# Attention values for 256 queries in one step, gate work at the end of a unit, expert gate-and-up weights in two halves

## The chip, the cores and the metric

One core of one Trainium2 chip runs the whole program. The metric is the device time of one execution in microseconds (us), lower is better. The engines are TensorE (PE, with its weight loads PEld), VectorE (DVE), ScalarE (ACT), GpSimd (POOL) and SyncE (SP), which issues the large transfers.

## What is computed

Two layers of a mixer block run on 512 rows of x and 256 rows of context, then a second block (dilated and forgetting attention, then a mixture of 32 experts). The change touches two parts. The first is the attention of the two mixer layers:

```python
def one_block(qi):                      # 128 queries; 8 heads
    s = jnp.einsum('bqhd,bkhd->bhqk', qi, k).astype(jnp.float32) * sm_scale
    p = jax.nn.softmax(s, axis=-1).astype(v.dtype)
    return jnp.einsum('bhqk,bkhd->bqhd', p, v)
...
y_a = attn * jax.nn.silu(g_a)
```

Its keys are the 256 context rows and the 512 rows of x; in layer 0 the context rows are queries too, against the context alone. The second is the experts:

```python
for e in range(N_EXPERTS):              # 32 experts, 1024 -> 256 -> 1024
    he = jax.nn.silu(xt @ w_gate[e]) * (xt @ w_up[e])
    y = y + combine[:, e:e + 1] * (he @ w_down[e])
```

## The kernel before

Every engine runs its own list of instructions in order, and all five lists come from one walk that each engine's code goes through with its own functions. Between engines there are counted semaphores; there is no scheduler, so the order in the walk is the order on the engine.

**Attention.** A *unit* is one head and 128 queries: five units per head in layer 0 (`per = 5`; the fifth, `i == 4`, is the 256 context queries against the 256 context keys) and four in layer 1; 40 and 32 units in all. `attention_walk` goes through the units u. For each it calls, in this order: `values` of an earlier unit if one is due at u, `turn_p(u)` (TensorE turns the softmax weights P, six transposes of 128x128, DVE and ACT copy them to PTa/PTb/PTc), a piece of turning the next heads' q or k, `normalise(u+2)` (DVE reciprocal, POOL multiply), `scores(u+3)` (TensorE q·k, DVE maximum, ACT exponential), and `finish` (DVE's low parts of turned q and k). Heads go in pairs, an even and an odd one. `values` multiplies PT with v for the two heads of a pair: the even head's result lands in rows 0 to 63 and the odd head's in rows 64 to 127 of one PSUM place, and the `due` table says at which unit each step stands. In `values`, DVE multiplies the place with the gate (L1687, into `og`), ACT copies the result to the high part `yax` or `yac` (L1634), and POOL makes the low part (L1717).

**PSUM places.** `K.G` is a ring of four places of 512 columns, made in `attention_pe`. Each P piece (two per unit, one for `i == 4`), each turned piece of q or k, and each step of values takes the next place in turn. A taker waits until the last user's reader is done: for a place of values that is DVE's gate multiplication, event `gated`. The scores have two places of their own, used alternately.

**Experts.** The experts go in 16 pairs. For a pair, TensorE multiplies 64 rows each with the gate-and-up weights `gu` (L3421, 8 row blocks k, two experts beside each other in the columns of the array), turns the result and multiplies with `dn` (L3444). Six `gu` buffers of 2 MB and eight `dn` buffers of 1 MB form rings. SP issues one transfer per buffer (`experts_load`), each after the last user is done (`weight_free`) and after the fourth load before it has landed.

Of the kernel before, what the change touches and what calls it, by code (L numbers as in the profile page):

```python
# [15 lines left out]
NX = 512  # L16
# [251 lines left out]
def setup(K, nc):  # L268
# [16 lines left out]
    for l, a in ((0, 0), (1, 50)):  # L285
# [14 lines left out]
            (f"P{l}", 4 * row, a + 30, a + 30), (f"PTa{l}", 12 * kb, a + 30, a + 30), (f"PTb{l}", 6 * kb, a + 30, a + 30),  # L300
            (f"PTc{l}", 4 * kb if l == 0 else 32, a + 30, a + 30), (f"og{l}", 3 * kb, a + 30, a + 30),
# [4 lines left out]
        if l == 0:  # L306
            items += [("zero", 4 * kb, 30, 30), ("yac0", 8 * kb, 30, 42), ("ysc0", 4 * kb, 20, 42), ("ypc0", 4 * kb, 24, 42)]
# [1105 lines left out]
def attention_walk(S, l, turn=nothing, rest=nothing, scores=nothing, normalise=nothing, turn_p=nothing, values=nothing):  # L1413
# [47 lines left out]
def attention_buffers(K, l):  # L1461
# [6 lines left out]
    A.P, A.PT = ring("P", 4, (NT,)), (ring("PTa", 4, (6, 128)), ring("PTb", 2, (6, 128)))  # L1468
    A.PTc = ring("PTc", 2, (2, 256)) if l == 0 else None
    A.gate = ring("og", 3, (256,))  # L1470
# [3 lines left out]
    def pt(u):  # L1474

        h, i = units[u]
        if i == 4:
            return A.PTc[h % 2], u - 2 * per + per * (1 - h % 2)
        if h % 2 == 0:
            return A.PT[0][i], u - per  # L1480
        return A.PT[1][i % 2], u - 2 if i >= 2 else u - 2 * per + 2
# [59 lines left out]
def attention_pe(S, l):  # L1541
# [40 lines left out]
    def values(u):  # L1582
        h, i = units[u]
        s, before = K.G.take("gated", l, u)
        n, kts = (128, range(6)) if i < 4 else (NC, (4, 5))
        for kt in kts:
            for odd in range(2):
                of = u - per * (1 - odd)
                o = 64 * (h - 1 + odd)
                for w in q(*[("pt", l, of, j) for j in range(len(A.jobs(of)))], *[("v", l, t) for t in range(6)], *before):  # L1590
# [11 lines left out]
def attention_act(S, l):  # L1602
# [25 lines left out]
    def values(u):  # L1628
        h, i = units[u]
        c, n = 128 * i % NX, 128 if i < 4 else NC  # L1630
# [4 lines left out]
    attention_walk(S, l, turn=turn, scores=scores, turn_p=turn_p, values=values)  # L1635
# [8 lines left out]
def gate_of(A, u):  # L1644

    h, i = A.units[u]
    return (h // 2 * A.per + i) % 3


def attention_dve(S, l):  # L1650
# [29 lines left out]
    def values(u):  # L1680
        h, i = units[u]
        c, n = 128 * i, 128 if i < 4 else NC
        g = gate_of(A, u)
        earlier = [v for v in range(u) if units[v][0] % 2 and gate_of(A, v) == g]
# [3 lines left out]
    attention_walk(S, l, rest=rest, scores=scores, normalise=normalise, turn_p=turn_p, values=values)  # L1688


def attention_pool(S, l):
# [3 lines left out]
    if l == 0:  # L1695
        zero = K.sb("zero", [128, D])
# [14 lines left out]
    def values(u):  # L1711
        h, i = units[u]
        c, n = 128 * i % NX, 128 if i < 4 else NC
# [4 lines left out]
    attention_walk(S, l, normalise=normalise, values=values)  # L1718


def attention_sp(S, l):
    K, e, q = S.K, S.e, S.q
    if l == 0:
        for w in q(("zeros",)):
            e.wait_ge(*w)
        e.dma_start(K.ybuf.rearrange("(p c) n -> p c n", c=8), K.sb("zero", [128, D])[:, :].unsqueeze(1).to_broadcast([128, 8, D])).then_inc(*q.land("zero"))
# [10 lines left out]
def y_ready(l, v, k, part):  # L1737
# [4 lines left out]
    return [(("yah", "yal")[part], l, per * (2 * k + 1) + i) for i in (range(4) if v == 0 else (4,))]  # L1742
# [1310 lines left out]
def experts_load(S, n):  # L3053
    K, e, q = S.K, S.e, S.q
    for i in range(S.loaded, S.loaded + n):
        w, x = EXPERT_LOADS[i]
        for s in q(*weight_free(w, x), *([("w", *EXPERT_LOADS[i - 4])] if i > 3 else [])):
            e.wait_ge(*s)
        b = weight_place(K, w, x)
        e.dma_start(b[:, :, :], K.d["w_" + w][x]).then_inc(*q.land_as(f"{w}{x % (N_GU if w == 'gu' else N_DN)}", "w", w, x))  # L3060
# [40 lines left out]
def weights_of(K, E, job):  # L3101

    kind, n = job
    if kind == "far":
        return [(E.w_gu, ("second.far_gu", n), E.w_dn, ("second.far_dn", n))]
    return [(weight_place(K, "gu", x), ("w", "gu", x), weight_place(K, "dn", x), ("w", "dn", x)) for x in (2 * n, 2 * n + 1)]
# [283 lines left out]
def experts_pe(S):  # L3390
# [21 lines left out]
    def up(job, xt, j, free):  # L3412
# [3 lines left out]
        for k in range(KT):  # L3416
            for i, (gu, loaded, _, _) in enumerate(ws):
                o = slice(n * i, n * i + n)
                for w in q(ev("XT", job, 0), ev("XT", job, 1), loaded, *before):
                    e.wait_ge(*w)  # L3420
                m = e.matmul(s[o, :], x[:, k, o], gu[:, k, :], start=k == 0, stop=k == KT - 1, skip_group_check=True)  # L3421
                if k == KT - 1 and i == len(ws) - 1:
                    m.then_inc(*q.up(*ev("up", job)))
# [479 lines left out]
```

## Time and profile before

| what | value |
|---|---|
| median of 3 runs | 1336.57 us (1335.91 to 1337.82) |
| profiled execution, its own time | 1337.34 us |
| its span in the trace | 1335.5 us |
| mean granted TensorE clock | 0.985 of full speed |
| busy: PE, DVE, ACT, POOL | 96%, 50%, 39%, 40% of the span |

The profile is of one execution; its own time is 0.77 us above the median. Busy time is what the hardware recorded on each engine. A matmul's end is modelled, and in an unbroken stream the next one starts before the modelled end of the last, so distances from start to start are the safer reading. An fp32 matmul shows as two records. The two attentions lie at about 280 to 391 us and 626 to 721 us, the experts at 1070 to 1306 us.

### The profile page before, as it was taken

How to read it: one execution, taken by the hardware profiler on the slowest of the kernel's cores; microseconds unless marked ns; L12 is line 12 of the kernel's file. 1: busy time of each engine (PE TensorE's matmuls, PEld its weight loads, DVE VectorE, ACT ScalarE, POOL GpSimd, SP SyncE). 2: the span in 40 equal slices, each digit the busy share in tenths (PEclk: the TensorE clock that was granted, in tenths of full speed). 3: DMA queues.
4: the chain of work that ended last, by engine and by line, in shares of the span. 5: the costliest groups of instructions: out<-in, count | busy, mean ns of one | idle time of the engine just before them, and what ended most of it. 6: DMA issues, size and time to landing. Idle time of an engine off the chain costs nothing. (4 is left out here: it accounts for less than half of the span.)

```text
span 1335.5 us, 20477 instructions
## 1 busy us (share of the span) xinstructions
PE 1277.2 (96%) x7788; PEld 925.0 (69%) x7788; DVE 662.2 (50%) x1358; ACT 524.9 (39%) x1121; POOL 538.9 (40%) x552
## 2 busy tenths in 40 slices
PE   7999999999999999999999999999989989989995
PEld 6766777878888878667888987767668933333332
DVE  5555995147741587973774331544454511111125
ACT  4312343357652344434665333655452221111111
POOL 0213698344445446874334521665261101111121
PEclk9999999999999999999999999999999799999998
DMA  9782111140013231022001222221046779999985
GB/s 395 302 295 95 48 47 48 48 158 2 1 48 111 80 117 63 32 79 80 2 1 47 82 95 87 81 102 48 32 158 254 297 291 419 422 419 416 418 346 210
DMA packets 42513, 209.58 MB, mean 157 GB/s; under 512 B 7255, under 2 KB 9687, under 8 KB 33184
## 3 DMA queue, kind: packets, MB, share of 16 engines
q1 hardware_dynamic: 34192, 194.59, 37.5%
q0 software_dynamic: 5760, 10.27, 2.1%
q10 hardware_dynamic: 2448, 3.21, 0.8%
q8 instruction: 71, 1.16, 0.4%
q14 instruction: 42, 0.34, 0.1%
HBM read 201.46 MB, written 17.30 MB: 164 GB/s over the span
## 5 line engine op out<-in xcount | busy, mean ns | idle before, releaser
L438 POOL TENSOR_TENSOR wlo<-raw,whi 128x512 fp32r<-128x512 f32 x102 | 141.3, 1389 | 140.8 <-ACT whi L426 135.8
L3421 PE MATMUL ps<-gu,XT 128*64 128x512 f32 x608 | 135.7, 595 | 8.6 <-DVE XT L3533 5.1
L426 ACT ACTIVATE whi<-raw 128x512 fp32r<-128x512 f32 x124 | 76.8, 629 | 149.1 <-PE ps L881 112.3
L1165 DVE SCALAR_TENSOR_TENSOR z<-glu,small,z 128x798 f32<-128x798 f32 (+1 forms) x120 | 132.5, 1153 | 0.8
L881 PE MATMUL ps<-hxh,whi 128*128 128x512 f32 x304 | 129.3, 425 | 0.5 <-ACT whi L426 0.5
L881 PE MATMUL ps<-hxh,wlo 128*128 128x512 f32 x304 | 120.1, 395 | 2.1 <-POOL wlo L438 2.1
L881 PE MATMUL ps<-hxl,whi 128*128 128x512 f32 x304 | 120.6, 397 | 0.0
L3421 PEld LDWEIGHTS ps<-gu,XT 128*64 128x64 f32 x608 | 45.0, 137 | 86.7 <-issue 75.9
L1708 POOL TENSOR_SCALAR P<-P,stat 128x768 f32<-128x768 f32 (+1 forms) x80 | 65.5, 821 | 72.2 <-DVE stat L1670 71.1
L1617 ACT ACTIVATE P<-ps,stat 128x768 f32<-128x768 f32 (+1 forms) x80 | 65.1, 814 | 59.0 <-DVE stat L1663 58.3
L1663 DVE TENSOR_REDUCE stat<-ps 128x1 f32<-128x768 f32 (+1 forms) x72 | 66.6, 925 | 22.5 <-PE ps L1568 22.2
L3538 DVE TENSOR_TENSOR he<-ps,he 128x256 f32<-128x256 f32 x19 | 8.1, 424 | 137.6 <-ACT he L3499 137.6
L881 PEld LDWEIGHTS ps<-hxh,whi 128*128 128x128 f32 x304 | 57.8, 190 | 22.9 <-issue 9.6
L3444 PE MATMUL ps<-dn,heT 128*64 128x512 f32 x304 | 69.4, 598 | 3.5 <-DVE heT L3543 3.5
L881 PEld LDWEIGHTS ps<-hxh,wlo 128*128 128x128 f32 x304 | 57.5, 189 | 15.6 <-POOL wlo L438 2.5
L881 PEld LDWEIGHTS ps<-hxl,whi 128*128 128x128 f32 x304 | 57.7, 190 | 14.1 <-issue 2.2
L3499 ACT ACTIVATE he<-ps 128x256 f32<-128x256 f32 x19 | 7.3, 383 | 149.8 <-PE ps L3421 149.8
L1578 PE MATMUL ps<-ident,P 128*128 128x128 f32 x416 | 61.3, 283 | 1.2 <-DVE qT_1l L1525 0.5
L3615 POOL DMA_INDIRECT h<-h2d,kept x16 | 16.3, 1020 | 110.8 <-PE ps L3408 77.1
L2525 POOL TENSOR_SCALAR P<-P,stat 128x128 f32<-128x128 f32 (+3 forms) x64 | 35.1, 559 | 49.9 <-DVE stat L2471 49.9
L2221 PE MATMUL ps<-hh,whi 128*128 128x512 f32 x128 | 55.1, 430 | 0.0
L1578 PEld LDWEIGHTS ps<-ident,P 128*128 128x128 f32 x416 | 47.4, 143 | 10.6 <-issue 5.9
(849 smaller groups left out, 3189.2 us busy)
## 6 DMA issues: line engine op xcount, KB each, us to landing
gu<-in_w_gu_dram SPq DMA_DIRECT2D x32, 2048.0 KB, 16.4
raw<-in_w_in_dram SPq DMA_DIRECT2D x66, 512.0 KB, 3.3
dn<-in_w_dn_dram SPq DMA_DIRECT2D x32, 1024.0 KB, 16.5
wgate<-in_w_mod_dram SPq DMA_DIRECT2D x16, 1024.0 KB, 7.8
raw<-in_w_out_dram SPq DMA_DIRECT2D x24, 512.0 KB, 3.2
wmod<-in_w_mod_dram SPq DMA_DIRECT2D x4, 2048.0 KB, 14.9
ybuf<-zero SPq DMA_DIRECT2D x1, 4096.0 KB, 12.7
yin<-ybuf SPq DMA_DIRECT2D x4, 1024.0 KB, 9.4
```

The lines of the kernel that those rows point to most:

```text
L426: e.activation(K.hi[i][:, half(h)], K.raw[i % 2][:, half(h)], ACT.Copy).then_inc(*q.up("hi", i, h))
L438: e.tensor_tensor(K.lo[i][:, half(h)], K.raw[i % 2][:, half(h)], K.hi[i][:, half(h)].bitcast(F32), ALU.subtract).then_inc(*q.up("lo", i, h))
L881: p = e.matmul(s[0:m, o:o + n], a, K.h[l, v][x][:, k, :], start=k == 0 and part == 0 and x == 0, stop=end)
L1165: e.scalar_tensor_tensor(o, x, weight, o, ALU.mult, ALU.add).then_inc(*q.up("conv", l, i, j))
L1578: m = e.transpose(s[:, 128 * j:128 * j + 128], A.P[u % 4][:, c:c + 128], K.ident[:, :])
L1617: e.activation(P[:, wide * j:wide * j + wide], s[:, wide * j:wide * j + wide], ACT.Exp, bias=K.stat[:, c0 + j:c0 + j + 1], accum_out=K.sta ...
L1663: e.tensor_reduce(stat[:, c0:c0 + n], A.S[u % 2][:, 0:n * wide].rearrange("p (n w) -> p n w", w=wide), AX.X, ALU.max, negate=True).then_in ...
L1708: e.tensor_scalar(P[:, wide * j:wide * j + wide], P[:, wide * j:wide * j + wide], K.stat[:, c0 + 4 + j:c0 + 5 + j], 0.0, ALU.mult, ALU.add ...
L2221: m = e.matmul(s[:, :], (K.hi, K.lo)[part][i][:, 128 * k:128 * k + 128], K.h[2, 0][x][:, k, :], start=k == 0 and part == 0 and x == 0, sto ...
L2525: e.tensor_scalar(P[:, 0:n], P[:, 0:n], stat[:, c0 + 3:c0 + 4], 0.0, ALU.mult, ALU.add).then_inc(*q.up("normal2", u))
L3421: m = e.matmul(s[o, :], x[:, k, o], gu[:, k, :], start=k == 0, stop=k == KT - 1, skip_group_check=True)
L3444: m = e.matmul(s[o, :], turned_of(E, job)[:, k, o], dn[:, k, 512 * c:512 * c + 512], start=k == 0, stop=k == 1, skip_group_check=True)
```

## The change

Four things are changed in the attentions, and one in the experts.

1. One step of `values` now serves two units, that is 256 queries: units i = 0 and 1, or i = 2 and 3 of both heads. The context unit i = 4 stays a step of its own. PT tiles are 256 queries wide (two for each head instead of 4 and 2 of 128), and so are the gate tiles `og`, two instead of three.
2. The steps stand at other units: at 8, 10 and 12 of each ten in layer 0 (before 6, 8, 10, 12 and 14), at 7 and 9 of each eight in layer 1 (before 5, 7, 9 and 10).
3. The gate work on DVE, ACT and POOL is no longer done where `values` stands, but by a new call `gate` after `scores(u+3)` of the same unit.
4. The tile of zeros is 256 columns wide instead of 1024, and its transfer reads it more often.
5. Each `gu` buffer is loaded by two transfers of 1 MB (row blocks 0 to 3, and 4 to 7). The first may start when the first half of the pair's multiplication is done (`up_half`), and the multiplication waits for each half by itself.

```diff
-            (f"P{l}", 4 * row, a + 30, a + 30), (f"PTa{l}", 12 * kb, a + 30, a + 30), (f"PTb{l}", 6 * kb, a + 30, a + 30),
-            (f"PTc{l}", 4 * kb if l == 0 else 32, a + 30, a + 30), (f"og{l}", 3 * kb, a + 30, a + 30),
+            (f"P{l}", 4 * row, a + 30, a + 30), (f"PTa{l}", 12 * kb, a + 30, a + 30), (f"PTb{l}", 12 * kb, a + 30, a + 30),
+            (f"PTc{l}", 4 * kb if l == 0 else 32, a + 30, a + 30), (f"og{l}", 2 * kb, a + 30, a + 30),
...
-    due = {2 * per * p + d: 2 * per * p + per + i for p in range(HEADS // 2) for i, d in enumerate((6, 8, 10, 12, 14) if l == 0 else (5, 7, 9, 10))}
+    due = {2 * per * p + d: 2 * per * p + per + i for p in range(HEADS // 2) for i, d in (((1, 8), (3, 10), (4, 12)) if l == 0 else ((1, 7), (3, 9)))}
...
-        if u in due:
-            values(due.pop(u))
+        own = due.pop(u, None)
+        if own is not None:
+            values(own)
         turn_p(u)
...
         if u + 3 < n:
             scores(u + 3)
+        if own is not None:
+            gate(own)
         finish()
     for u in sorted(due):
         values(due[u])
+        gate(due[u])
...
+def value_part(A, u):
+    i = A.units[u][1]
+    return (128 * i - 128, 256, [u - 1, u]) if i < 4 else (NX, NC, [u])
...
-        n, kts = (128, range(6)) if i < 4 else (NC, (4, 5))
+        kts = range(6) if i < 4 else (4, 5)
+        _, n, own = value_part(A, u)
         for kt in kts:
             for odd in range(2):
-                of = u - per * (1 - odd)
+                of = [v - per * (1 - odd) for v in own]
+                p = A.PT[odd][i // 2] if i < 4 else A.PTc[odd]
...
-                m = e.matmul(s[64 * odd:64 * odd + 64, 0:n], B.vN[:, kt, o:o + 64], A.pt(of)[0][:, kt - kts[0], :],
+                m = e.matmul(s[64 * odd:64 * odd + 64, 0:n], B.vN[:, kt, o:o + 64], p[:, kt - kts[0], :],
...
-    attention_walk(S, l, rest=rest, scores=scores, normalise=normalise, turn_p=turn_p, values=values)
+    attention_walk(S, l, rest=rest, scores=scores, normalise=normalise, turn_p=turn_p, gate=values)
...
-def weight_free(w, x):
+def weight_free(w, x, part=1):
+    up = ("up_half", "up")[part]
...
-        return [("first.up", p), ("second.up", p)] if w == "gu" else [("first.down", p, 1), ("second.down", p, 1)]
+        return [("first." + up, p), ("second." + up, p)] if w == "gu" else [("first.down", p, 1), ("second.down", p, 1)]
...
+        rows = slice(KT // 2 * part, KT // 2 * part + KT // 2)
+        e.dma_start(b[:, rows, :], K.d["w_gu"][x][:, rows, :]).then_inc(*q.land_as(f"gate{x % N_GU}" if part == 0 else f"gu{x % N_GU}", *(("w", "gu", x) if part else ("w_half", "gu", x))))
...
-                for w in q(ev("XT", job, 0), ev("XT", job, 1), loaded, *before):
+                for w in q(ev("XT", job, 0), ev("XT", job, 1), loaded[k // (KT // 2)], *before):
```

On DVE, in layer 0, this stood in unit 8, which begins with a step of values (`og0_1` is the gate tile, `PTb0_1` the copy of the unit's P, `stat_60` holds reciprocal and maximum, `kT0_1l` a turned piece of k):

```order
L1687 TENSOR_TENSOR og0_1_240<-ps,ga0_214 128x128 [waits s_pe_attention]
L1678 COPY PTb0_1_236<-ps 128x512 [waits s_pe_attention]
L1670 RECIPROCAL stat_60<-stat_60 128x1 [waits s_act_attention]
L1663 TENSOR_REDUCE stat_60<-ps 128x1 [waits s_pool_attention,s_pe_attention]
L1525 SCALAR_TENSOR_TENSOR kT0_1l_226<-ps,small_54,kT0_1h_225 96x512 [waits s_act_attention]
```

and this stands there now:

```order
L1690 COPY PTb0_1_234<-ps 128x4x128 [waits s_pe_attention]
L1682 RECIPROCAL stat_60<-stat_60 128x1 [waits s_act_attention]
L1675 TENSOR_REDUCE stat_60<-ps 128x1 [waits s_pool_attention,s_pe_attention]
L1699 TENSOR_TENSOR og0_0_237<-ps,ga0_214 128x256
L1528 SCALAR_TENSOR_TENSOR kT0_1l_226<-ps,small_54,kT0_1h_225 96x512 [waits s_act_attention]
```

The gate multiplication moved from the unit's beginning to behind the maximum of scores(u+3), and is twice as wide.

TensorE's list from the end of that step of values into unit 9 reads now as follows (L1597 values, L1581 transposes of P, L1505 transposes of k, L1571 scores; each piece of P or k takes one of the four places):

```order
L1597 MATMUL ps<-PTb0_0_233,vN0_218 64x256
L1581 MATMUL ps<-ident_49,P0_0_227 128x128 [waits s_dve_attention,s_pool_attention]
L1581 MATMUL ps<-ident_49,P0_0_227 128x128 x3
L1581 MATMUL ps<-ident_49,P0_0_227 128x128 [waits s_act_attention]
L1581 MATMUL ps<-ident_49,P0_0_227 128x128
L1505 MATMUL ps<-ident_49,kN0_217 96x128 [waits s_dve_attention]
...
L1571 MATMUL ps<-kT0_0h_223,qT0_0l_220 128x512
L1571 MATMUL ps<-kT0_0h_223,qT0_0l_220 128x256
L1581 MATMUL ps<-ident_49,P0_1_228 128x128 [waits s_dve_attention,s_pool_attention]
```

The rows are those of before but for the 256 columns of the values; what moved is the instruction behind the last wait on DVE: the transposes of P0_1 take the fourth place after the values, which is the values' own, and its reader is now the gate multiplication at the end of unit 8.

SP's list of loads in the experts had, where the rings begin to be reused:

```order
L3060 DMA gu0_348<-in_w_gu_dram 128x4096 [waits s_gu4,s_pe_second,s_pe_first]
L3060 DMA gu1_350<-in_w_gu_dram 128x4096 [waits s_dn6]
L3060 DMA gu2_352<-in_w_gu_dram 128x4096 [waits s_gu5,s_pe_second,s_pe_first]
L3060 DMA gu3_354<-in_w_gu_dram 128x4096 [waits s_dn7]
L3060 DMA dn0_349<-in_w_dn_dram 128x2048 [waits s_gu0,s_pe_second,s_pe_first]
```

and has now:

```order
L3082 DMA gu0_342<-in_w_gu_dram 128x2048 [waits s_gu4,s_pe_second,s_pe_first]
L3082 DMA gu1_344<-in_w_gu_dram 128x2048 [waits s_dn6]
L3082 DMA gu0_342<-in_w_gu_dram 128x2048 [waits s_pe_second,s_pe_first]
L3082 DMA gu1_344<-in_w_gu_dram 128x2048
L3082 DMA gu2_346<-in_w_gu_dram 128x2048 [waits s_gu5,s_pe_second,s_pe_first]
```

Both first halves of a pair go ahead of both second halves.

## Rows read from the trace of the kernel before

**Rows 1.** The page: busy time of the engines; TensorE's granted clock.

```profile
PE 1277.2 (96%) x7788; PEld 925.0 (69%) x7788; DVE 662.2 (50%) x1358; ACT 524.9 (39%) x1121; POOL 538.9 (40%) x552
...
PEclk9999999999999999999999999999999799999998
```

**Rows 2.** Windows: 20 units of layer 0, 16 units of layer 1.

```profile
core 0: us, PE busy (x) PEld busy (x) DVE busy (x) ACT busy (x) POOL busy (x), PEclk, DMA share, GB/s
300.43:354.50 54.07, 53.41 (x490) 46.32 (x489) 40.62 (x85) 37.94 (x95) 23.26 (x34) 1.00 0.01 2
644.69:690.25 45.56, 45.29 (x426) 39.48 (x425) 33.66 (x68) 30.07 (x69) 18.19 (x25) 1.00 0.01 1
```

**Rows 3.** Timeline of PE: values for 128 and for the context.

```profile
start us, us, engine line op out<-in xcount [idle before <-releaser]
305.69 0.51 PE L1568 MATMUL ps<-kT_0h,qT_0l 96*128 96x512 f32 x2
306.13 0.32 PE L1592 MATMUL ps<-PTa,vN 128*64 128x128 f32 x1
...
307.59 0.87 PE L1578 MATMUL ps<-ident,P 128*128 128x128 f32 x6
...
322.60 1.08 PE L1592 MATMUL ps<-PTc,vN 128*64 128x256 f32 x8
323.61 0.66 PE L1578 MATMUL ps<-ident,P 128*128 128x128 f32 x4
```

**Rows 4.** Waits before L1592 (all its steps), and one such step on PE.

```profile
  ACT PTb L1626: 3.7, 8
...
711.49 0.43 PE L1592 MATMUL ps<-PTa,vN 128*64 128x128 f32 x2
712.68 0.29 PE L1592 MATMUL ps<-PTb,vN 128*64 128x128 f32 x1 [0.76 <-ACT PTb L1626]
...
714.11 0.33 PE L1578 MATMUL ps<-ident,P 128*128 128x128 f32 x1
```

**Rows 5.** Timeline of PE and of DVE where scores end.

```profile
309.44 0.51 PE L1568 MATMUL ps<-kT_0h,qT_0l 96*128 96x512 f32 x2
309.79 0.60 PE L1578 MATMUL ps<-ident,P 128*128 128x128 f32 x4
310.23 0.38 PE L1502 MATMUL ps<-ident,kN 128*96 128x128 f32 x2
...
309.99 0.96 DVE L1663 TENSOR_REDUCE stat<-ps 128x1 f32<-128x768 f32 x1 [0.94 <-PE ps L1568]
```

**Rows 6.** Groups by line and form on DVE: gate and maximum.

```profile
L1687 DVE TENSOR_TENSOR og<-ps,ga 128x128 f32<-128x128 f32 x32 | 9.1, 286 | 11.1 <-PE ps L1592 11.1
L1687 DVE TENSOR_TENSOR og<-ps,ga 128x256 f32<-128x256 f32 x4 | 1.7, 416 | 0.6 <-PE ps L1592 0.6
L1663 DVE TENSOR_REDUCE stat<-ps 128x1 f32<-128x768 f32 x64 | 61.1, 954 | 21.2 <-PE ps L1568 20.8 <-issue 0.3
```

**Rows 7.** The chain that ended last: from DVE's end to TensorE's start.

```profile
1309.23 0.43 DVE heT L3543
1309.66 0.04 issue
1309.71 3.68 PE ps L3444 x16
```

**Rows 8.** Windows around two idle stretches of TensorE; columns as in rows 2.

```profile
286.00:289.00 3.00, 1.66 (x10) 1.09 (x8) 1.94 (x4) 1.19 (x3) 0.90 (x1) 1.00 1.02 412
289.00:293.00 4.00, 3.51 (x20) 3.46 (x19) 3.27 (x8) 2.54 (x6) 1.25 (x2) 0.57 1.03 417
...
1179.00:1182.00 3.00, 0.55 (x3) 0.20 (x4) 0.06 (x1) 0.00 (x0) 1.01 (x1) 1.00 1.02 419
1182.00:1185.00 3.00, 3.00 (x16) 1.01 (x14) 0.00 (x0) 0.00 (x0) 0.00 (x0) 1.00 1.01 419
```

**Rows 9.** Experts: a wait of PE, windows as in rows 2, and dn's transfers.

```profile
1181.75 7.08 PE L3421 MATMUL ps<-gu,XT 128*64 128x512 f32 x30 [2.45 <-DMA gu<-in_w_gu_dram]
...
1023.00:1034.00 11.00, 11.00 (x70) 9.78 (x69) 7.47 (x34) 3.33 (x8) 1.34 (x3) 1.00 1.01 419
1092.00:1290.00 198.00, 190.54 (x916) 69.23 (x914) 33.99 (x63) 34.22 (x92) 30.52 (x33) 1.00 1.01 415
...
1022.26 11.67 SPq L3060 DMA_DIRECT2D dn<-in_w_dn_dram  x4
```

More of the change, by code:

```diff
@@ L1410, in turn_pieces, with attention_walk @@
     return [(1, 0), (1, 4), (0, 0)] + ([(0, 4)] if l == 0 else [])
-def attention_walk(S, l, turn=nothing, rest=nothing, scores=nothing, normalise=nothing, turn_p=nothing, values=nothing):
+def attention_walk(S, l, turn=nothing, rest=nothing, scores=nothing, normalise=nothing, turn_p=nothing, values=nothing, gate=nothing):
     per, units, due = attention_order(l)
@@ L1467, in attention_buffers @@
     A.qT, A.kT = ([[K.sb(f"{name}{l}_{b}{p}", [128, n], F32R) for p in "hl"] for b in range(2)] for name, n in (("qT", n_own), ("kT", NT)))
-    A.P, A.PT = ring("P", 4, (NT,)), (ring("PTa", 4, (6, 128)), ring("PTb", 2, (6, 128)))
+    A.P, A.PT = ring("P", 4, (NT,)), (ring("PTa", 2, (6, 256)), ring("PTb", 2, (6, 256)))
     A.PTc = ring("PTc", 2, (2, 256)) if l == 0 else None
-    A.gate = ring("og", 3, (256,))
+    A.gate = ring("og", 2, (256,))
     A.S = K.bank.get(("places of scores", l))
@@ L1629, in values @@
         h, i = units[u]
-        c, n = 128 * i % NX, 128 if i < 4 else NC
+        c, n, _ = value_part(A, u)
+        c %= NX
         hi, _ = K.y[l, i // 4, h // 2]
@@ L1634, in values @@
         e.activation(hi[:, c:c + n], A.gate[gate_of(A, u)][:, 0:n], ACT.Copy).then_inc(*q.up("yah", l, u))
-    attention_walk(S, l, turn=turn, scores=scores, turn_p=turn_p, values=values)
+    attention_walk(S, l, turn=turn, scores=scores, turn_p=turn_p, gate=values)
 def pt_free(A, l, u):
@@ L1681, in values @@
         h, i = units[u]
-        c, n = 128 * i, 128 if i < 4 else NC
+        c, n, _ = value_part(A, u)
         g = gate_of(A, u)
-        earlier = [v for v in range(u) if units[v][0] % 2 and gate_of(A, v) == g]
+        earlier = [v for v in range(u) if units[v][0] % 2 and units[v][1] in (1, 3, 4) and gate_of(A, v) == g]
         for w in q(("values", l, u), ("ev", l, AT["ga", h // 2]), *([("yah", l, earlier[-1]), ("yal", l, earlier[-1])] if earlier else [])):
@@ L1717, in values @@
         e.tensor_tensor(lo, A.gate[gate_of(A, u)][:, 0:n], hi.bitcast(F32), ALU.subtract).then_inc(*q.up("yal", l, u))
-    attention_walk(S, l, normalise=normalise, values=values)
+    attention_walk(S, l, normalise=normalise, gate=values)
 def attention_sp(S, l):
@@ L1741, in y_ready @@
     per, units, _ = attention_order(l)
-    return [(("yah", "yal")[part], l, per * (2 * k + 1) + i) for i in (range(4) if v == 0 else (4,))]
+    return [(("yah", "yal")[part], l, per * (2 * k + 1) + i) for i in ((1, 3) if v == 0 else (4,))]
 def out_walk(S, l, product=nothing, step=nothing, h_steps=None, middle=nothing):
@@ L3054, in experts_load @@
     K, e, q = S.K, S.e, S.q
[L3055 removed]
+    done = range(S.loaded, S.loaded + n)
+    halves = [(i, part) for part in range(2) for i in done if EXPERT_LOADS[i][0] == "gu"]
+    if any(EXPERT_LOADS[i][1] < N_GU for i, _ in halves):
+        halves.sort()
+    for i, part in halves + [(i, 1) for i in done if EXPERT_LOADS[i][0] == "dn"] if len(halves) in (0, 2 * n) else sorted(halves + [(i, 1) for i in done if EXPERT_LOADS[i][0] == "dn"]):
         w, x = EXPERT_LOADS[i]
[L3057 removed]
+        for s in q(*weight_free(w, x, part), *([("w", *EXPERT_LOADS[i - 4])] if i > 3 else [])):
             e.wait_ge(*s)
         b = weight_place(K, w, x)
[L3060 removed]
+        if w == "dn":
+            e.dma_start(b[:, :, :], K.d["w_dn"][x]).then_inc(*q.land_as(f"dn{x % N_DN}", "w", "dn", x))
+            continue
+        rows = slice(KT // 2 * part, KT // 2 * part + KT // 2)
+        e.dma_start(b[:, rows, :], K.d["w_gu"][x][:, rows, :]).then_inc(*q.land_as(f"gate{x % N_GU}" if part == 0 else f"gu{x % N_GU}", *(("w", "gu", x) if part else ("w_half", "gu", x))))
     S.loaded += n
```

26 lines of the change are left out of this document (13 added, 13 removed).

## The prediction

> **What bounds the kernel now.** I read the page first. TensorE is busy 96% of the span at nearly full clock, the other engines 39 to 50% [rows 1], so the question for each stretch is what TensorE does or waits for there. The windows of the two attentions say the same: TensorE is busy 53.41 of 54.07 us over 20 units of layer 0 and 45.29 of 45.56 us over 16 units of layer 1, so 2.7 and 2.85 us a unit, while DVE has 2.03 and 2.10 us of work in each [rows 2]. A microsecond that TensorE saves there is a microsecond of the whole, and so is one that it waits. In the experts TensorE is busy 190.5 of 198 us; the transfers run at 415 GB/s the whole time, yet they hold TensorE up clearly at one place only, for 2.45 us [rows 9].
>
> **The steps of values.** A step for 128 queries takes 1.46 us from its first matmul to the next instruction, and starts 0.44 us after the last pair of scores records, where a transpose starts 0.35 us after it (309.44 to 309.79): 0.09 us more on the way in [rows 3, 5]. A transpose of 128 columns takes 0.11 us (four in 0.44) [rows 5]. The step has 12 pairs of records, the two of a pair run beside each other, so 12 x 0.11 = 1.32 us is streaming and 0.14 us is fixed. The context step with its 256 columns and 4 pairs takes 1.01 us [rows 3], (1.01 - 0.14) / 4 = 0.22 us a pair. So 256 columns stream no faster than 2 x 128. A step for 256 queries should take 12 x 0.2175 + 0.14 = 2.75 us, with the way in 2.84 us, and two steps of before take 2 x 1.55 = 3.10 us. There were 32 such steps, there are now 16: **-16 x 0.26 = -4.2 us**. Bounds: if nothing of the fixed part is saved, 0; if 0.35 us a step is, -5.6 us.
>
> **The waits for PT.** Of all things that TensorE waits for in front of values, the largest is the ACT copy of the youngest P into PTb, 3.7 us in 8 times; at 711.49 us the step starts with PTa and stands 0.76 us for PTb, and lasts 2.62 instead of 1.46 us [rows 4]. The new steps stand one unit farther behind the units that they use (units 6, 8 and 9 of ten at 8, 10 and 12), so those copies are long done: **-3.7 us**, between -1 (if the other copies are as late somewhere else) and -4.7. It comes back at the two ends. There the last step of 256 queries follows right on the transposes of its own last unit, where before another step of 128 stood between; it waits for a copy as in rows 4, about 0.75 us in each layer: **+1.5 us**, bounds 0 and +3.
>
> **The gate work behind scores(u+3).** This is the term that decides. What costs is not the gate work itself: DVE does 128x256 in 0.416 us where it did 128x128 twice for 0.286 each [rows 6], ACT and POOL have time. It is when the values' PSUM place comes free. The ring has four places. After a step of values in unit u the takers are: P's two pieces, a turned piece of q or k if the unit has one, then P's first piece of unit u+1. With a turned piece, that first piece is the fourth taker and gets the values' own place; without one, the second piece does. Its reader is the gate multiplication, which on DVE now stands behind the maximum of scores(u+3), and these scores are the last thing that TensorE does before it wants the place. Before, the gate multiplication stood ahead of unit u's copies and was done two microseconds earlier, so this wait cost nothing. The cover is gone, and the price from rows is: after TensorE's last scores record it would go on at 309.79, and DVE starts the maximum at 309.99, so 0.20 us [rows 5]; the maximum 0.95 us, the gate for 256 columns 0.42 us [rows 6]; from DVE's end to TensorE's start 0.05 us (1309.66 to 1309.71) [rows 7]. Together **1.62 us** in which TensorE has nothing ahead of the wait to do. Where it is the second piece that waits, the four transposes of the first run before it, 0.44 us, and 1.18 us are left.
>
> How often: in layer 0 units 8, 18, 28 (i = 3) and 10, 20, 30 (i = 0) have a turned piece, units 12, 22, 32 have none; unit 38 has no scores(u+3) behind it and costs nothing. In layer 1 units 7, 15, 23 have one, 9, 17, 25 have none; 31 is like 38. So 6 + 3 = 9 waits of 1.62 us and 3 + 3 = 6 of 1.18 us: 14.6 + 7.1 = **+21.7 us**. Queued behind the waiting transposes are all of unit u+1's scores, and DVE, ACT and POOL wait for these in turn, so nobody overtakes. Bounds: the wait can't be shorter than DVE's two operations less 0.44, 0.93 us, so 15 x 0.93 = 14; with 0.3 us more each for restarting TensorE and for DVE's other work, 26.
>
> **The clock.** TensorE's granted clock fell to half at one such place: in 286 to 289 us it was busy 1.66 of 3 us, and over the next 4 us the granted clock was 0.57, a loss of 4 x 0.43 = 1.7 us. It did not fall where TensorE was busy 0.55 of 3 us at 1179 [rows 8]. A new wait of 1.62 us is of this size, and between them TensorE is busy without a gap. I take two falls in the nine longer waits, **+3.4 us**, bounds none and seven (+12).
>
> **Six units without values.** In layer 0 units 13 to 17 and in layer 1 units 10 to 14 of each round now have no step of values. DVE's work a unit, less the gate's, is 1.9 to 2 us [rows 2, 6], and TensorE's without values is about 2, so they run level; I take 0, up to +3.
>
> **The halves of gate and up.** With the first half's transfer free to start at the middle of a multiplication of 7.08 us [rows 9], the train of loads starts up to 3.5 us earlier, and the multiplication can start when two quarters of the pair's bytes are still on their way. Either is more than the 2.45 us of waiting at 1181.75: **-2.45 us**, at most -2.8, at least 0 (if another load is late in its place). What it adds, 26 and more SP instructions, lies beside transfers that keep SP waiting anyway. Are transfers of 1 MB slower than 2 MB? The dn loads are 1 MB with 8 KB a row, as the halves will be, and four of them ran at 419 GB/s, against 415 for the mix [rows 9]: no cost, the value I take. The Trainium skill says otherwise: DMA: Bandwidth & Descriptors, section Bandwidth, gives 341 GB/s for 1 MB and 425 for 16 MB and asks for 1 MiB or more. That is for one transfer by itself; with four in the queue this trace does not agree. By that page the 198 us of loads would become, as an estimate of mine from its two figures on two thirds of the bytes, 198 x (425/341 - 1) x 2/3 = 33 us longer.
>
> The smaller tile of zeros and its transfer lie beside the start of attention 0, off TensorE's path: 0.
>
> **The sum.** 21.7 + 1.5 + 3.4 - 4.2 - 3.7 - 2.45 = +16.3 us on the profiled execution's own 1337.34 us, so 1353.6 us. That execution was 0.77 us above the median of the runs, so I forecast **1353 us**, 1.2% slower.
>
> **Rivals.**
> 1. *The waits for the place do not exist or are hidden*, and only the savings are left: 4.2 + 3.7 + 2.45 = 10.35, 1336.57 - 10.35 = 1326 us, faster. It would need the place to be free when asked for. It decides when a wait costs less than (4.2 + 3.7 + 2.45) / 15 = 0.7 us each on average. For it speaks only that TensorE could find its next P late there anyway; against it that after 309.44 the transposes start without a gap [rows 5], so P is ready. 5%.
> 2. *Part of the price comes back*: while TensorE waits, the others catch up and later small waits go, or the run of units without values absorbs it. At half of 21.7 us: 1342 us (1339 to 1346). Against it: there is only 0.7 us of TensorE idle in 54 us to be given back [rows 2]. 11%.
> 3. *The clock falls after most of the waits*, five or more times: 1353 + (5 to 8 less 2) x 1.7 = 1358 to 1364 us, and more with DVE running level. 14%.
> 4. *The halves' stream is slower*, so that the experts become bound by transfers. TensorE has 7.5 us of slack in 198 [rows 9], so 10% less speed would cost some 12 us: 1365 us. 2%. This is what the page named above would lead to.
> 5. *Savings and waits cancel* within 2.7 us: 2%.
>
> My own sum, with none to four falls and the bounds above, holds 66%: 1346 to 1358 us.
>
> **Chances and range.** A measurement of this kernel can tell 0.2%, 2.7 us, from no change. Slower: 66 + 14 + 10 (of the 11) + 2 = 92%. Same: 2 + 1 = 3%. Faster: 5%. The range 1343 to 1363 us holds the likeliest case and about half of the second and two thirds of the third; outside lie rival 1, the fourth, the rest of those, and a little of the first.
>
> **What the new profile would show.** (a) On TensorE, waits of 1.3 to 1.6 us before the transposes of P with DVE's gate multiplication as the releaser, nine times, and of about 1.1 us six times. (b) Steps of values 2.7 to 2.8 us long and without waits for PTb, but for the last in each layer. (c) The two attentions together 14 to 22 us longer, with PEclk digits below 9 where the clock fell. (d) In the experts no idle on gu, and these 2 to 3 us shorter, at 415 GB/s. I would be wrong if DVE's gate did not release those transposes, if TensorE were waiting there for something else already, or if the experts changed by more than 3 us.

## The result and the profile after

The changed kernel takes **1357.97 us** (median of 4 runs, 1355.17 to 1358.93) where the kernel before took 1337.19 us in the same comparison (4 runs, 1335.91 to 1338.46): ratio 1.0156, 95% interval 1.0136 to 1.0176, so 1.6% slower, 20.8 us. The forecast was 1353 us in a range of 1343 to 1363. The profiled execution took 1358.93 us, its span is 1356.9 us. In the experiments further down two far slower runs are left out of all figures: one of the kernel before (4091.88 us) and one of four of the kernel without the halves (4438.57 us).

The page of the changed kernel, as in [rows 1]:

```profile
PE 1276.0 (94%) x7404; PEld 904.8 (67%) x7404; DVE 656.9 (48%) x1342; ACT 524.5 (39%) x1105; POOL 536.2 (40%) x536
PEclk9999999999999999999999999999999999999998
```

TensorE is busy as long as before to 1.2 us and the span is 21.4 us longer: what came in is waiting, not work. The windows lie over the same 20 units of layer 0 and 16 units of layer 1 as [rows 2]; the third is three microseconds around one of the new waits:

```profile
core 0: us, PE busy (x) PEld busy (x) DVE busy (x) ACT busy (x) POOL busy (x), PEclk, DMA share, GB/s
302.33:364.43 62.10, 53.59 (x393) 42.03 (x392) 39.36 (x80) 37.42 (x89) 22.62 (x30) 1.00 0.00 1
663.09:714.07 50.98, 45.45 (x329) 35.65 (x328) 33.21 (x65) 30.09 (x65) 17.43 (x20) 1.00 0.00 1
...
307.00:310.00 3.00, 1.53 (x12) 1.20 (x11) 2.11 (x4) 1.65 (x5) 0.62 (x2) 1.00 0.00 0
```

The same units take 62.10 instead of 54.07 us and 50.98 instead of 45.56 us. The list of what TensorE waited for, over the whole span (us in total, how many times, the longest), has a first line that the kernel before does not have at all:

```profile
PE ps L1581 <- DVE og L1699: 18.9, 15, 1.5
```

One such wait in the timelines of TensorE and DVE; the turned piece of k stands between scores(u+3) and them as in [rows 5]:

```profile
306.93 0.51 PE L1571 MATMUL ps<-kT_0h,qT_0l 96*128 96x512 f32 x2
308.91 0.63 PE L1581 MATMUL ps<-ident,P 128*128 128x128 f32 x4 [1.47 <-DVE og L1699]
...
307.47 0.96 DVE L1675 TENSOR_REDUCE stat<-ps 128x1 f32<-128x768 f32 x1 [0.94 <-PE ps L1571]
308.35 0.41 DVE L1699 TENSOR_TENSOR og<-ps,ga 128x256 f32<-128x256 f32 x1
```

TensorE's last scores record starts at 306.93 and the transposes at 308.91, 1.98 us later, where [rows 5] had 0.35: 1.63 us, nine times. DVE is in the maximum and then in the gate multiplication the whole time. Where four transposes stand ahead, it reads so:

```profile
321.81 0.60 PE L1581 MATMUL ps<-ident,P 128*128 128x128 f32 x4
323.35 0.44 PE L1581 MATMUL ps<-ident,P 128*128 128x128 f32 x2 [0.94 <-DVE og L1699]
```

1.54 us from start to start instead of 0.44: 1.10 us, and over the six of them 1.10 to 1.25 us. These distances from start to start are 0.16 us longer than the idle time in the lists, which counts from the modelled end of the record before.

From the first scores to the first product behind an attention, start to start, layer 0 takes 123.66 us (277.92 to 401.58; before 280.20 to 391.52, 111.32), layer 1 takes 105.97 us (639.59 to 745.56; before 625.71 to 720.60, 94.89). The two attentions are 23.4 us longer. These two distances are what the experiments below are compared by. The stretches before, between and behind them, up to the experts, differ by -2.3, +3.8 and -2.7 us between these two traces, with falls of the granted clock at different times in them; no experiment looks at those.

In the experts the stall of [rows 9] is gone; the same multiplication in the timeline of TensorE:

```profile
1201.84 7.09 PE L3443 MATMUL ps<-gu,XT 128*64 128x512 f32 x32
1208.85 1.09 PE L3430 MATMUL ps<-ident,xg 128*128 128x128 f32 x8
```

and the window of the 198 us that answers to that of [rows 9], columns as above:

```profile
1114.00:1312.00 198.00, 192.99 (x932) 70.35 (x930) 34.14 (x63) 35.02 (x93) 30.59 (x33) 1.00 1.01 407
```

From the first gate-and-up record to the last down record the experts take 241.2 us instead of 242.1, only 0.9 us less, although the stall of 3.52 us is gone. The first pair takes 1.4 us more (36.97 instead of 35.61 us to the second): the granted clock is at half speed for a while from 1092.3 on. The kernel without the halves has that fall too (1092.1), so it does not come of them.

### The profile page after: what moved, and what is told of

It is laid out like the page before. It is cut to its first block and busy times, and to the rows that moved or that the text cites. A ratio compares the mean times of both kernels' runs of the same rounds, so it can differ in the third digit from the quotient of the medians.

```text
span 1356.9 us, 19681 instructions
## 1 busy us (share of the span) xinstructions
PE 1276.0 (94%) x7404; PEld 904.8 (67%) x7404; DVE 656.9 (48%) x1342; ACT 524.5 (39%) x1105; POOL 536.2 (40%) x536
## 5 line engine op out<-in xcount | busy, mean ns | idle before, releaser
L1581 PE MATMUL ps<-ident,P 128*128 128x128 f32 x416 | 62.6, 281 | 22.9 <-DVE og L1699 18.9
L1675 DVE TENSOR_REDUCE stat<-ps 128x1 f32<-128x768 f32 (+1 forms) x72 | 66.5, 924 | 30.0 <-PE ps L1571 29.6
L1581 PEld LDWEIGHTS ps<-ident,P 128*128 128x128 f32 x416 | 46.2, 142 | 39.8 <-issue 22.0
L3637 POOL DMA_INDIRECT h<-h2d,kept x16 | 16.4, 1024 | 110.2 <-PE ps L3430 76.9
```

The costliest lines, as they stand in the source:

```text
L1581: m = e.transpose(s[:, 128 * j:128 * j + 128], A.P[u % 4][:, c:c + 128], K.ident[:, :])
L1675: e.tensor_reduce(stat[:, c0:c0 + n], A.S[u % 2][:, 0:n * wide].rearrange("p (n w) -> p n w", w=wide), AX.X, ALU.max, negate=True).then_in ...
```

## The experiments

The theory: DVE's gate multiplication is late by its place in DVE's list, and what it holds back is TensorE's fourth taker of the PSUM ring. The main rivals: the chain of maximum, exponential and normalisation is too slow for TensorE anyway; or the wide steps cost by themselves. Times of the kernel before in the same comparisons were 1338.6 to 1340.2 us.

**The gate directly behind the values.** In the walk:

```diff
         if own is not None:
             values(own)
+            gate(own)
         turn_p(u)
...
-        if own is not None:
-            gate(own)
         finish()
```

> The changed kernel, but the gate work of a step of values stands directly behind it again (DVE, ACT and POOL, in every unit), with nothing else undone. Theory of the place: the 15 waits of TensorE before the transposes of P, from start to start 1.63 us each nine times and 1.1 to 1.25 us six times, 22 us together, are gone, because the gate multiplication is done while TensorE turns P; 1358 - 22 = 1336 us, and no wait on the gate multiplication is left but the one behind the last scores of layer 0. Rival, the chain of one unit behind the other (maximum, exponential, normalise) is too slow for TensorE whoever frees the place: TensorE waits for POOL or ACT in the same spots, and the time stays over 1345 us.

1339.13 us (12 runs), ratio 0.9993, interval 0.9977 to 1.0009. All waits on the gate multiplication are gone; layer 0 takes 111.15 us, layer 1 96.34 us, together 22.1 us less than in the changed kernel. These are the gate's place, but for 1.7 us that the changed kernel's trace lost to the clock at the end of layer 1 (further down), and no wait of TensorE came up in their stead. But this kernel still has wide steps and halves, and it is no faster than before: that is the next question.

**The gate ahead of scores(u+3).**

```diff
+        if own is not None:
+            gate(own)
         if u + 3 < n:
             scores(u + 3)
-        if own is not None:
-            gate(own)
```

> The changed kernel, with the gate work ahead of scores(u+3) instead of behind it: still at the end of the unit, behind the copies of P and the reciprocal, but ahead of the maximum. Theory of the place: what costs is only that the maximum of scores(u+3) stands ahead; DVE is idle for 0.94 us before that maximum, the gate multiplication of 0.41 us fits in, and the 22 us are gone as with the gate directly behind the values: 1336 us, within 2 us of that kernel. Rival, any gate work away from the step of values is late: over 1345 us.

1337.78 us (12 runs), ratio 0.9976 (0.9957 to 0.9994); layer 0 111.28, layer 1 96.14 us. DVE's timeline there:

```profile
307.31 0.69 DVE L1690 COPY PTb<-ps 128x512 f32<-128x512 f32 x1 [2.12 <-PE ps L1581]
307.92 0.15 DVE L1682 RECIPROCAL stat<-stat 128x1 f32<-128x1 f32 x1
307.99 0.41 DVE L1699 TENSOR_TENSOR og<-ps,ga 128x256 f32<-128x256 f32 x1
```

The gate work falls into the time in which DVE waits for the scores. So it may stand late in the unit; only the maximum must not stand ahead of it.

**The halves alone,** on the kernel before, with all of the change in the experts' functions:

```diff
-        e.dma_start(b[:, :, :], K.d["w_" + w][x])
+        rows = slice(KT // 2 * part, KT // 2 * part + KT // 2)
+        e.dma_start(b[:, rows, :], K.d["w_gu"][x][:, rows, :])
...
-                for w in q(ev("XT", job, 0), ev("XT", job, 1), loaded, *before):
+                for w in q(ev("XT", job, 0), ev("XT", job, 1), loaded[k // (KT // 2)], *before):
```

> The kernel before with only the gate-and-up weights loaded as two halves. From start to start the one stall on gu cost 3.5 us in the trace of before (two records took 3.52 us, the multiplication 10.54 instead of 7.02 us), its idle time as listed is 2.45 us. By start to start: 1337.2 - 3.5 = 1333.7 us; by the idle time, as in the prediction, 1334.7 us. Rival, halves stream more slowly: no gain or slower than 1337, with the transfers under 400 GB/s.

1335.54 us (12 runs), ratio 0.9971 (0.9956 to 0.9986), 3.9 us faster. No wait on gu is left. The timing holds both expectations; that the stall was 3.52 us is read from the trace of before, where the multiplication started at 1178.23 and went on, in its stream, only at 1181.75.

**The values' place passed over.** The gate stays last; the order in which places are taken changes:

```diff
+    def hold(self, *event):
+        first = self.places[0][1]
+        if first and first[0][0] == "gated" and self.passed.get(first[0], 0) < 2 and event[0] == "pt":
+            self.passed[first[0]] = self.passed.get(first[0], 0) + 1
+            self.places[0], self.places[1] = self.places[1], self.places[0]
+        return Ring.hold(self, *event)
```

> The changed kernel, its gate work at the end of the unit as it is; only the order in which TensorE takes the four places is changed: a piece of P that would get the values' place before the gate multiplication is done takes the next place, up to twice. The place is then taken later, mostly by the piece of q or k turned after both pieces of P, some 0.66 us behind. Theory of the place: each wait moves behind these transposes and shortens from 1.63 or 1.1 us to about 0.97 us, 13 or 14 of them, 13 instead of 22 us: 1349 us. Rival, DVE's lateness holds TensorE up in another way than by the place: no change, 1358 us.

1350.57 us (5 runs), ratio 1.0090 (1.0070 to 1.0110): by the traces the two attentions take 219.7 us, 12.2 us more than with the gate first (13 expected), where the changed kernel, without its loss to the clock, has 20.4 us more. So 8 us of the price are gone, with DVE's list as in the changed kernel. The lines of waits of layer 0 and of layer 1:

```profile
PE ps L1516 <- DVE og L1710: 6.5, 8, 0.9
...
PE ps L1516 <- DVE og L1710: 3.6, 5, 0.7
```

Thirteen waits moved from the transposes of P to those of q and k behind them and became shorter. What holds TensorE up is the place.

**The gate last, with steps of 128 queries.** The kernel before with only the new call:

```diff
-        if u in due:
-            values(due.pop(u))
+        own = due.pop(u, None)
+        if own is not None:
+            values(own)
         turn_p(u)
...
             scores(u + 3)
+        if own is not None:
+            gate(own)
         finish()
```

> The kernel before, steps of values for 128 queries, the old table, no halves; only the gate work stands at the end of the unit, behind scores(u+3). Theory of the place: what costs is the gate's place in DVE's list, not the width of the steps, and with more steps there are more waits: 14 places in layer 0 and 9 in layer 1 where the fourth taker comes with nothing (14 times) or four transposes (9 times) in between; the gate multiplication is 0.13 us shorter, so 14 x 1.50 + 9 x 1.05 = 30 us over the kernel before, about 1367 to 1371 us. Rival, the waits come of the wide steps (a place held for 2.75 instead of 1.46 us): then less than 10 us over the kernel before.

1370.64 us (4 runs), ratio 1.0242 (1.0220 to 1.0264): 32 us, where 30 were expected; the two attentions are 29.6 us longer by the trace. The list has 15 waits of 16.1 us in total in layer 0 and 10 of 10.3 us in layer 1. That is two waits more than were counted, both short (0.54 and 0.34 us). The late gate costs more with narrow steps, because there are more of them.

**The steps spread over the units,** with the gate first:

```diff
-(((1, 8), (3, 10), (4, 12)) if l == 0 else ((1, 7), (3, 9)))
+(((1, 8), (3, 11), (4, 14)) if l == 0 else ((1, 7), (3, 10)))
```

> Steps of 256 queries with the gate work directly behind the values, as in the run with the gate first, and only the table changed: steps at units 8, 11 and 14 of ten in layer 0 and 7 and 10 of eight in layer 1, so that no more than three units in a row (layer 0) have no step of values. In the run with the gate first TensorE lost 0.52 us in a wait for the copy into PTb and about 0.4 us in slower scores and transposes per ten units, in the run of five units without values. Theory, there the softmax chain sets the pace: these 0.9 us a round come back, 2.7 us in layer 0 and 0.5 to 1 us in layer 1: 3 us under the run with the gate first, 0.3 to 0.4 per cent under the kernel before. Rival, it is something else than the bare units: no difference to the run with the gate first.

1337.97 us (12 runs), ratio 0.9993 (0.9978 to 1.0009). Layer 0 takes 110.08 us, 1.1 less than with the gate first, layer 1 97.41, 1.1 more. Neither theory: the bare run of units was part of it in layer 0, and in layer 1 the later step cost as much.

**The last pair of heads in steps of 128,** on top of that:

```diff
+    wide, narrow = (((1, 8), (3, 11), (4, 14)), (6, 8, 10, 12, 14)) if l == 0 else (((1, 7), (3, 10)), (5, 7, 9, 10))
+    due = {2 * per * p + d: 2 * per * p + per + i for p in range(HEADS // 2) for i, d in (wide if p < HEADS // 2 - 1 else enumerate(narrow))}
```

> The spread table and the gate first, and for the last pair of heads of each layer the steps of 128 queries and the table of before. Theory of the tail: behind the last scores TensorE has no values to do while POOL normalises and ACT copies; in layer 1 it waited 1.21 and 0.51 us there and steps of 256 queries start later. With narrow steps that is as before, a wait of 0.76 us for PTb, and layer 1 ends 1 to 1.5 us earlier than with the spread table alone, layer 0 about the same: 1 to 2 us under it, 0.4 to 0.5 per cent under the kernel before. Rival, the narrow steps' own fixed cost eats it: no difference.

1338.03 us (12 runs), ratio 0.9997 (0.9983 to 1.0011). Layer 1 takes 96.44 us, 1.0 less, layer 0 110.70, 0.6 more. The wide ending does cost in layer 1; over both layers it is 0.35 us, which no timing here can tell.

**The attention part without the halves:** the changed kernel with the two lines above, and what belongs to them, as before:

```diff
-                for w in q(ev("XT", job, 0), ev("XT", job, 1), loaded[k // (KT // 2)], *before):
+                for w in q(ev("XT", job, 0), ev("XT", job, 1), loaded, *before):
```

> The changed kernel without the halves: the attention part of the change alone. Theory: the two parts add up; the halves were worth 3.5 to 4 us by themselves, so the attention part alone costs what the whole change costs plus that, 24 to 25 us over the kernel before (ratio about 1.0185), with the stall of 3.5 us on gu back in the experts. Rival, they interact (the shifted start of the experts alone hides the stall): the ratio of the changed kernel, 1.0156.

1359.99 us (3 runs), ratio 1.0153 (1.0126 to 1.0181), the expected 1.0185 just outside, the ratio of the whole change inside. Layer 0 takes 123.83 and layer 1 103.94 us, 2.0 us less than in the changed kernel. In its trace the stall on gu is back, smaller than before: the multiplication starts at 1201.02 and goes on, in its stream, at 1203.71, 2.69 us. So the halves are worth 2.7 us in the changed kernel by the trace; the timing, with its interval of 7 us, says neither.

**Two passes of 128 columns in one step,** on the kernel with the gate first:

```diff
+        half = [(0, 128), (128, 256)] if i < 4 else [(0, n)]
+        for kt, (c0, c1) in [(kt, c) for c in half for kt in kts]:
```

> As the run with the gate first (steps at the same units, one PSUM place a step), but each step for 256 queries is made of two passes of 128 columns, one behind the other: the width alone is undone. By the model of the prediction a step of 256 columns takes 12 x 0.2175 + 0.14 = 2.75 us and two passes 24 x 0.11 + 0.14 = 2.78 us, plus at most another 0.14 us where the second pass begins: 2.8 to 2.9 us from first matmul to next instruction. So the width by itself is worth 0.03 to 0.17 us a step, what was saved is the number of steps, and the attentions are 0.5 to 2.7 us longer. Rival, narrow matmuls are dearer: a step of 3.1 us or more.

1342.37 us (one run). Every undisturbed step takes 2.77 us, against 2.74 to 2.75 us in one pass; layer 0 111.42 and layer 1 96.63 us, 0.3 us more each. The width by itself is worth some 0.02 us a step. What two steps of 1.46 us lose against one is a step's own beginning and end.

**Wide steps in layer 0 only,** spread table, gate first, halves:

```diff
-for i, d in (((1, 8), (3, 10), (4, 12)) if l == 0 else ((1, 7), (3, 9)))}
+for i, d in (((1, 8), (3, 11), (4, 14)) if l == 0 else enumerate((5, 7, 9, 10)))}
...
+    return (128 * i - 128, 256, [u - 1, u]) if A.per == 5 else (128 * i, 128, [u])
```

> Each stage with what did best in the traces: halves in the experts; layer 0 with steps of 256 queries, the spread table and the gate first; layer 1 with steps of 128 queries and its table of before. From the traces, first scores to first product behind: layer 0 110.1 us (before 111.3), layer 1 94.9 (before 94.9; with wide steps 96.3 to 97.4), experts 3.9 us under before. Sum 5.1 us under the kernel before, ratio 0.996, and 1 us under the halves alone. Rival, the gain in layer 0 is not there without the wide layer 1: then the ratio of the halves alone, 0.997.

**1333.01 us** (7 runs), ratio 0.9951 (0.9933 to 0.9968): faster than both kernels. Layer 0 109.95, layer 1 94.94 us, as taken from the traces. The expected 0.996 lies inside. Whether it is also faster than the halves alone (0.9971) the timing leaves open: their interval begins at 0.9956 and overlaps this one. The traces say that layer 0 is 1.4 us shorter.

**A step at unit 7 instead of 6,** narrow steps, halves:

```diff
-enumerate((6, 8, 10, 12, 14) if l == 0
+enumerate((7, 8, 10, 12, 14) if l == 0
```

> The kernel before with the halves, and in layer 0 the first of the five steps of values at unit 7 of ten instead of 6, with nothing wider. There TensorE stood in front of the youngest copy into PTb, 0.47 to 0.9 us from start to start in each of four rounds. Theory A, that wait was part of the pace of the softmax chain: it comes back elsewhere, layer 0 stays at 111.3 us within 0.5, and time is that of the halves alone. Theory B, it is a loss of its own: layer 0 takes 2.65 us less, 108.7 us. The savings of the wide steps came back in full, so I hold A for likelier, 65 to 35.

1336.46 us (12 runs), ratio 0.9970 (0.9953 to 0.9987), that of the halves alone. Layer 0 takes 109.89 us: of 2.65 us in front of PTb 1.4 came through. I held that nothing would; it is half. No step waits for PTb any more, and at 301.83 the transposes of P do:

```profile
300.92 0.60 PE L1578 MATMUL ps<-ident,P 128*128 128x128 f32 x4
301.83 0.44 PE L1578 MATMUL ps<-ident,P 128*128 128x128 f32 x2 [0.30 <-ACT PTb L1626]
```

**Halves loaded, both awaited.**

```diff
-    return [(weight_place(K, "gu", x), [("w_half", "gu", x), ("w", "gu", x)], weight_place(K, "dn", x), ("w", "dn", x)) for x in (2 * n, 2 * n + 1)]
+    return [(weight_place(K, "gu", x), [("w", "gu", x)] * 2, weight_place(K, "dn", x), ("w", "dn", x)) for x in (2 * n, 2 * n + 1)]
```

> The kernel before with the halves loaded as in the change, but each multiplication waits for both halves of its weights before its first row block: what is left is only that the first half's transfer may start at the middle of an earlier multiplication. The stall of before was 3.52 us from start to start at one place. Theory, the earlier start does it (up to 3.5 us earlier): the multiplication there takes 7.02 us and starts without a gap, or with less than 0.5 us. Rival, the wait by halves does it: a stall of 1.7 us or more is left.

1333.98 us (one run). The stall of before is gone, but another stands at the end of the stage, where before and the halves alone have none:

```profile
1276.73 1.07 PE L3430 MATMUL ps<-gu,XT 128*64 128x512 f32 x2
1278.87 6.65 PE L3430 MATMUL ps<-gu,XT 128*64 128x512 f32 x29 [1.07 <-DMA gu<-in_w_gu_dram]
```

2.1 us from start to start. So the earlier start removes the first stall, and the wait by halves the second. The second rests on this one trace; for the first, the three kernels without halves (before, gate last with 128, no halves) all have that stall, and the eleven with them have none there.

## Why the prediction was right, and where it was not

**The waits for the place** were right in kind, number and size: nine of 1.63 us (predicted 1.62) and six of 1.10 to 1.25 (1.18), on the named transposes, with the named releaser. Added from start to start they are 21.9 us (21.7). The kernel with the gate first has 22.1 us less in the two attentions, of which 1.7 are the clock's (below), so the waits cost 20.4 us net, and 1.5 us came back in the units behind them: scores behind such a wait took 0.88 us where they took 1.08. The nearness of 22.1 and 21.9 is chance. Rival 1 is ruled out, and rival 2, which wanted half of the price back, too.

**The steps** take 2.74 to 2.75 us (2.75). The reason given for it held: 256 columns stream as 2 x 128, as the two passes show, and what is saved is the fixed part of a step.

**The step that failed is "Six units without values ... I take 0"**, with the two savings that it let stand. I took -4.2 us from fewer steps, -3.7 from PTb and +1.5 at the ends, -6.4 together. With the gate first nothing else of the attention part is left, and the attentions are 1.3 us *longer* than before (-0.2 and +1.45). The savings were there and were given back: over ten units of layer 0, the steps take 6.51 instead of 7.32 us and the way into them 0.18 less, but the ten units 26.81 instead of 26.87 us. I had looked at DVE's work in a unit and not at ACT's. Timeline of ACT and of TensorE in a unit without values that has a piece of q to turn, gate first:

```profile
326.84 0.90 ACT L1621 ACTIVATE P<-ps,stat 128x768 f32<-128x768 f32 x1 [0.88 <-DVE stat L1674]
327.63 0.19 ACT L1621 ACTIVATION_READ_ACCUMULATOR P<-ps,stat 128x1 f32 x1
327.73 0.59 ACT L1630 ACTIVATE PTb<-ps 128x512 f32<-128x512 f32 x1
328.20 0.68 ACT L1516 ACTIVATE qT_0h<-ps,stat 96x512 fp32r<-96x512 f32 x1
328.93 0.90 ACT L1621 ACTIVATE P<-ps,stat 128x768 f32<-128x768 f32 x1
...
327.47 0.60 PE L1580 MATMUL ps<-ident,P 128*128 128x128 f32 x4
328.37 0.44 PE L1580 MATMUL ps<-ident,P 128*128 128x128 f32 x2 [0.30 <-ACT PTb L1630]
```

From one exponential to the next ACT has 2.09 us (326.84 to 328.93) and no gap. TensorE's own work in a unit without values and with a piece of q is 1.93 us where nothing holds it up (scores 1.13, transposes of P 0.66, piece of q 0.14, from start to start). The next piece of P can't be turned before ACT has copied the last: 0.90 us from start to start instead of 0.44, and the scores behind are slower too (1.03 instead of 0.80 us). The same wait appears in the kernel with a step at unit 7, which has no wide step. That ACT's queue is the cause is read from these rows and not tested by a run of its own; that leaving units bare costs is shown in layer 0 by the spread table (1.1 us back) and by the step at unit 7 (1.25 of 2.65 us lost).

**The ends.** In layer 0 the last wide step lasts 3.10 us instead of 2.74. In layer 1 TensorE waits twice, the first time for POOL's normalisation, which I had not named:

```profile
735.61 0.88 PE L1581 MATMUL ps<-ident,P 128*128 128x128 f32 x6 [1.21 <-POOL P L1720]
736.99 0.45 PE L1597 MATMUL ps<-PTa,vN 128*64 128x256 f32 x1 [0.51 <-ACT PTb L1631]
```

The windows there, columns as above:

```profile
735.00:738.00 3.00, 1.89 (x12) 1.30 (x14) 1.50 (x4) 1.75 (x4) 1.46 (x2) 0.88 0.03 5
738.00:741.00 3.00, 3.00 (x18) 1.75 (x16) 0.00 (x0) 0.00 (x0) 0.00 (x0) 0.55 0.00 0
```

The granted clock falls there (0.88, then 0.55 of full speed), and behind none of the fifteen waits. The step of values in it runs at half pace, 4.43 us from start to start where the kernel without the halves takes 2.74, so this fall cost **1.7 us**. That kernel has the same two waits, as long and as far apart, and kept its clock; its windows there:

```profile
735.75:738.75 3.00, 1.89 (x16) 1.37 (x18) 1.50 (x4) 1.75 (x4) 1.44 (x2) 1.00 0.00 0
738.75:741.75 3.00, 3.00 (x26) 1.73 (x22) 0.37 (x2) 0.58 (x1) 0.00 (x0) 1.00 0.02 5
```

So did the kernels with the gate first, before the scores, with the spread table and in two passes: in one trace of six the clock fell there. **+3.4 us was wrong**: of the waits that the term counted none lowered the clock, and the 1.7 us came at another place, in this trace and not in its likes. Rival 3 is ruled out with it. Counted over both attentions the clock fell twice before and twice after; the others stand at the starts of the layers.

**The halves** were worth more than -2.45 us. I took the idle time as listed; the multiplication of [rows 9] had begun with two records of the pair's first expert (1178.23), which ran while the second expert's weights were missing. Elsewhere they run beside the second expert's records and cost nothing of their own, so the 1.07 us that they show as busy are lost as well. From start to start it is 3.52 us. The Trainium skill says in Perfetto Trace Analysis, section Tensor Engine Instruction, that the end of a TensorE instruction is an estimate and not observed. This trace agrees: the last of the two records is 0.59 us long, where in the unbroken stream the next pair starts after 0.43, but that is 0.16 of the 1.07 us.

**Rival 4, slower halves,** was right in sign and harmless. With 1 MB transfers only, 198 us of the experts ran at 403 to 408 GB/s in the eleven kernels with halves, with 2 MB transfers among them at 415 to 417 in the three without: 2% less. DMA: Bandwidth & Descriptors of the Trainium skill, section Bandwidth, has the sign, and its 341 GB/s for 1 MB is far from what several of them in the queue reach here.

The sum with measured terms: 20.4 (place) + 1.7 (clock) + 1.3 (steps, PTb, bare units and ends together) - 2.7 to -3.5 (halves) = 19.9 to 20.7 us; measured 20.8, interval 18.2 to 23.5. That the two agree so well is in part luck, as the stages that no experiment looked at differ by a few us each way between the traces. The forecast of +16.3 came 4.5 us short, because errors partly cancelled: +7.7 us (bare units and ends), -1.7 (clock), -1.3 (what came back of the waits), -0.3 to -1 (halves). Two signs of the list were missed: (c) had the attentions 14 to 22 us longer, they are 23.4, and (d) had the experts 2 to 3 us shorter at 415 GB/s, where the stall's 3.52 us are gone but a fall of the clock at the start takes 1.4 back, at 407 GB/s. The smaller tile of zeros, put at 0, no run tests by itself.

## What to carry to other kernels

A reader of a PSUM place may stand late in its engine's list, but not behind an operation that waits for the producer's newest work: count the takers of the ring up to the one that gets the place back, and see what the producer has left to do by then. When a kernel bound by one engine has fixed work per unit, taking that engine's work out of some units only pays, as the rows of ACT suggest here, as long as the next engine's work in just those units is shorter; look at the unit with the most side work, on every engine, not at means. Read stalls of TensorE from start to start, up to the next instruction of another kind: records that run alone ahead of a stall look like work. And before a difference between two traces is given to one cause, look in both for falls of the clock.

## What the runs showed of the hardware

- Single waits in an otherwise full stretch did not lower TensorE's clock: none of the 68 waits on the gate multiplication in four kernels (15, 15, 13 and 25; 0.3 to 1.5 us as listed) was followed by a lower granted clock. Behind two waits close together (1.21 and 0.51 us) with 1.89 us busy in 3 it fell to 1.2 GHz in one trace and stayed at 2.4 GHz in five others. What decides, these runs do not show.
- What a fall costs depends on where it lies. At 737 us it cost 1.7 us: a step of values took 4.43 instead of 2.74 us. At the start of layer 0 it cost nothing: 111.32 us in the kernel before with a fall (289 us), and 111.33 and 111.32 us without one, in the halves alone and with both halves awaited. At the start of layer 1 it cost 0.3 us: from the fourth unit on, the scores stood that much later in the changed kernel (fall at 648 us) than in the one without the halves, which has no fall there.
- The fp32 values multiplication takes the same time for 256 columns and for two passes of 128: 2.75 and 2.77 us.
